# Two weight buffers become one with high and low parts in alternate elements, and the operands beside it move to chosen offsets

## The chip, the cores and the metric

The kernel runs on one core of one Trainium2 chip. The metric is the device time of one execution in microseconds. The kernel before took 3037.07 us, the median of 3 runs (3036.71 to 3037.24).

## The reference

Two transformer-like blocks are computed in float32 for 256 tokens of width 1024, each with two layers. The first block carries a second stream of 256 context tokens; its layers are feed-forward, mixer (a Fourier and gated linear attention mixer in layer 0, a convolution and differential attention mixer in layer 1), feed-forward. The second block has one stream; each of its layers has four branches (state space, three kinds of attention), each projected by `w_branch`, gated by a sigmoid of `h @ w_gate`, summed, projected by `w_out`, and then a feed-forward. Almost all arithmetic is in products of activations with large weight matrices:

```python
def _swiglu(h, w_in, w_out):
    g, u = jnp.split(h @ w_in, 2, axis=-1)
    return (jax.nn.silu(g) * u) @ w_out

proj = jnp.einsum('bsnc,ncd->bsnd', ys, w_branch)
gates = jax.nn.sigmoid(h @ w_gate + b_gate).reshape(bsz, seq, N_BRANCH, D_MODEL)
merged = jnp.sum(gates * proj, axis=2)
return merged @ w_out
```

## The kernel before, in words

Every large product is made from two parts of each operand. A float32 number is split into a high part, rounded to the type fp32r, and a low part, the rest. `three` (L451) then issues three matmuls per tile: high by high, high by low, low by high. Each has its own stationary operand, 128 by 128, and a moving operand of 256 or 512 columns.

Weights come in units of at most 2048 elements per partition. There are two slots (index `s`), each of two halves of 1024 elements (index `h`), so a half holds up to eight tiles of 128 columns and feeds 24 matmuls. For each half, SyncE issues one DMA of up to 512 KB into `raw` (`sp_units`, L372), ScalarE copies it to `whi` (`act_split`, L396), VectorE writes `raw - whi` to `wlo` (`dve_split`, L402), and TensorE multiplies (`pe_blocks`, `pe_tokens`, `beside_block`, `product` and others, all through `half_of`, L457, and `three`). Semaphores count halves: ScalarE may overwrite a half of a slot when TensorE has finished the unit that used it (`mm_done`), DMA may overwrite `raw` when VectorE has made the low part (`lo_ready`).

In most products the weights are the stationary operand and the activations move. In the token-major ones (`pe_tokens`, the "v" units of `beside_block`, L1158, L1408) it is the other way round: the activations are stationary and 256 columns of weights move.

The activations are in three pairs of buffers: `xh`/`xl` (the inputs of the products after a norm or a mixer; 512 elements a row of `k`), `hid_h`/`hid_l` (the hidden layer of a feed-forward) and `h_yh`/`h_yl` (the branch outputs of the second block, 256 elements a row). ScalarE writes the high ones, VectorE the low ones.

All buffers are cut from one slab by hand: a `Region` (L132) hands out addresses one after the other, rounded up to 32 bytes. From the sizes, the buffers of this kernel stand at these bytes of the slab, and at these remainders of 512:

```
whi 43520 (0)   wlo 59904 (0)   hT 76288 (0)   xh 92672 (0)   xl 109056 (0)
hid_h 125440 (0)   hid_l 150016 (0)   h_yh 126112 (160)   h_yl 130208 (160)
```

All tiles of one buffer that a matmul takes (128 or 256 elements on, 2048 bytes on for the next `k` of `xh`) begin at the remainder of their buffer.

Of the kernel before, what the change touches and what calls it, by code (L numbers as in the profile page):

```python
# [20 lines left out]
F32R = mybir.dt.float32r  # L21
# [5 lines left out]
P = 128  # L27
D = 1024
DC = D // P
T = 256  # L30
# [3 lines left out]
UNIT = 2048  # L34
# [88 lines left out]
def build(nc, io, const_at):  # L123

    ctx = ExitStack()
    with ctx:

        SLAB = 212704
        base = (nc.sbuf_base + 31) // 32 * 32
        ctx.enter_context(nc.sbuf_tensor("slab", [P, SLAB // 4], F32))  # L130

        class Region:  # L132
# [5 lines left out]
            def __call__(self, name, shape, dt=F32):  # L138
# [2 lines left out]
                assert self.at <= self.end, (name, self.at, self.end)  # L141
                return t

        fixed = Region(0)
        n_const = max(b for _, b in const_at.values())
        consts = fixed("consts", [P, n_const])
# [14 lines left out]
        post_eps = rstd_col[:, NT:2 * NT]  # L161
        tok_scale = ss[:, T:2 * T]
        raw = fixed("raw", [P, 2, 2, UNIT // 2])
        whi = fixed("whi", [P, 2, 2, UNIT // 2], F32R)
        wlo = fixed("wlo", [P, 2, 2, UNIT // 2], F32R)
        hT = fixed("hT", [P, DC, 2 * T])
        xh_at = fixed.at
        xh = fixed("xh", [P, DC, 2 * T], F32R)
        xl_at = fixed.at
        xl = fixed("xl", [P, DC, 2 * T], F32R)  # L170
        overlay = fixed.at

        first = Region(overlay)
        hid_h = first("hid_h", [P, max(HALVES), 2 * T], F32R)
        hid_l = first("hid_l", [P, max(HALVES), 2 * T], F32R)
        act32 = first("act32", [P, 2, 2 * T])
        hid32 = first("hid32", [P, 2, 2 * T])
        out_at = first.at
        mod_w = first("mod_w", [P, 2, DC, 2 * P])
        mod_row = first("mod_row", [P, 2 * P])  # L180
# [40 lines left out]
        e_kkT0 = ev("e_kkT0", [P, 2, NT, 384])  # L221
        e_S = ev("e_S", [P, 2, 5, 3, P])
        e_xh = Region(xh_at, xl_at)("e_xh", [P, DC, 2 * T])
        e_xl = Region(xl_at, overlay)("e_xl", [P, DC, 2 * T])


        od = Region(overlay + 4 * DC * 2 * T)
# [16 lines left out]
        h_out = Region(out_at)("h_out", [P, DC, T])  # L244
        hy = Region(overlay)
        h_small = hy("h_small", [P, NT, 84])
        h_yh = hy("h_yh", [P, 4, T], F32R)
        h_yl = hy("h_yl", [P, 4, T], F32R)
        h_gates = hy("h_gates", [P, DC, T])
# [3354 lines left out]
```

## Time and profile before

| | before |
|---|---|
| median of 3 runs | 3037.07 us |
| span of the profiled execution | 3035.4 us |
| TensorE busy, matmuls | 2979.4 us (98%) |
| TensorE busy, weight loads | 2629.2 us (87%) |
| VectorE busy | 1691.5 us (56%) |
| ScalarE busy | 1314.2 us (43%) |
| DMA, mean | 145 GB/s |
| mean granted TensorE clock | 0.996 |

The span goes from the first to the last instruction of the core. Busy time of TensorE is modelled: each matmul has a length that includes the way through the array, so consecutive ones overlap, and how often they come is read from their starts. The profile gives no device time of the profiled execution besides its span.

### The profile page before, as it was taken

To read this page: it belongs to the slowest core of one execution; us is meant where nothing else is said; L and a number is where in the kernel's file an instruction comes from. 1 tells how busy PE (TensorE), PEld (TensorE's weight loads), DVE (VectorE), ACT (ScalarE), POOL (GpSimd) and SP (SyncE) were. 2 spreads that over 40 slices of the span, in tenths; PEclk is the share of its full clock that TensorE was granted. 3 is DMA by queue.
4 is the path that set the end of the run, shared out by engine and by line. 5 is a ranking of instruction groups with operands and counts; after the bars stand their busy time and mean duration, and the time that the engine had idled before them with its cause. 6 is when DMAs were issued, how large, how long until landed. Compare 5 with 4: busy or idle time off the path is not lost.

```text
span 3035.4 us, 52037 instructions
## 1 busy us (share of the span) xinstructions
PE 2979.4 (98%) x20172; PEld 2629.2 (87%) x20172; DVE 1691.5 (56%) x2664; ACT 1314.2 (43%) x1952; POOL 0.2 (0%) x4
## 2 busy tenths in 40 slices
PE   8999999999999999999999999999999999999999
PEld 6778878787777878888889999999899999998998
DVE  4333363544332453334666667677766676787666
ACT  4322333423222332223345555555654554556544
POOL 0000000000000000000000000000000000000000
PEclk9999999999999999999999999999999999999999
DMA  9564342055576433333324655455456645554564
GB/s 276 174 185 133 115 146 82 30 167 167 172 212 184 132 100 88 110 90 92 110 71 117 188 167 158 144 155 166 133 159 181 180 124 163 155 155 142 155 183 129
DMA packets 639011, 439.36 MB, mean 145 GB/s; under 512 B 22172, under 2 KB 627192, under 8 KB 638712
## 3 DMA queue, kind: packets, MB, share of 16 engines
q1 hardware_dynamic: 637844, 436.70, 48.3%
q8 instruction: 125, 2.05, 0.3%
q14 instruction: 46, 0.38, 0.0%
q10 hardware_dynamic: 996, 0.23, 0.0%
HBM read 430.84 MB, written 1.05 MB: 142 GB/s over the span
## 4 chain that ended last, share of the span: by engine, by line
PE 88%; DVE 7%; ACT 2%; issue 1%; SPq 1%; DMA 1%; DVEq 0%; ACTq 0%
PE ps L453 27%; PE ps L455 26%; PE ps L454 26%; PE ps L541 2%; DVE wlo L402 2%; ACT whi L396 1%; PE ps L1803 1%; PE ps L1771 1%; DMA raw<-ffn_w_in 1%; DVE normed L2666 1%; PE ps L1791 1%; SPq L717 1%; DVE xl L2658 0%; PE ps L1252 0%; PE ps L1261 0%
## 5 line engine op out<-in xcount | busy, mean ns | idle before, releaser
L453 PE MATMUL ps<-xh,whi 128*128 128x256 f32 (+1 forms) x3744 | 1218.3, 325 | 23.1 <-DVE wlo L402 5.1
L454 PE MATMUL ps<-xl,whi 128*128 128x256 f32 (+1 forms) x3744 | 1197.2, 320 | 0.0
L455 PE MATMUL ps<-xh,wlo 128*128 128x256 f32 (+1 forms) x3744 | 1197.1, 320 | 0.0
L402 DVE TENSOR_TENSOR wlo<-raw,whi 128x1024 fp32r<-128x1024 f32 x732 | 868.9, 1221 | 186.9 <-ACT whi L396 178.2
L396 ACT ACTIVATE whi<-raw 128x1024 fp32r<-128x1024 f32 x731 | 746.5, 1052 | 472.2 <-PE ps L455 412.6
L453 PEld LDWEIGHTS ps<-xh,whi 128*128 128x128 f32 x3744 | 713.8, 191 | 105.3 <-issue 43.4
L455 PEld LDWEIGHTS ps<-xh,wlo 128*128 128x128 f32 x3744 | 714.0, 191 | 50.8
L454 PEld LDWEIGHTS ps<-xl,whi 128*128 128x128 f32 x3744 | 714.7, 191 | 48.8
L453 PE MATMUL ps<-hid_h,whi 128*128 128x512 f32 (+1 forms) x1056 | 355.9, 337 | 0.0
L454 PE MATMUL ps<-hid_l,whi 128*128 128x512 f32 (+1 forms) x1056 | 354.9, 336 | 0.0
L455 PE MATMUL ps<-hid_h,wlo 128*128 128x512 f32 (+1 forms) x1056 | 354.8, 336 | 0.0
L2731 DVE TENSOR_TENSOR hid<-act,ps 128x512 f32<-128x512 f32 (+1 forms) x132 | 73.1, 554 | 460.7 <-PE ps L455 455.5
L2050 ACT ACTIVATE hid_h<-hid 128x256 f32 (+3 forms) x132 | 69.3, 525 | 445.8 <-DVE hid L2731 445.8
L453 PEld LDWEIGHTS ps<-hid_h,whi 128*128 128x128 f32 x1056 | 200.4, 190 | 23.5 <-issue 3.3
L455 PEld LDWEIGHTS ps<-hid_h,wlo 128*128 128x128 f32 x1056 | 200.5, 190 | 20.7
L454 PEld LDWEIGHTS ps<-hid_l,whi 128*128 128x128 f32 x1056 | 200.5, 190 | 20.4
L2782 DVE SCALAR_TENSOR_TENSOR hT<-ps,mod,hT 128x256 f32 (+1 forms) x112 | 49.9, 480 | 214.9 <-PE ps L455 214.6
L2735 DVE TENSOR_TENSOR hid_l<-hid,hid_h 128x256 f32 (+3 forms) x132 | 73.8, 559 | 105.7 <-ACT hid_h L2050 105.7
L2047 ACT ACTIVATE act<-ps 128x512 f32<-128x512 f32 (+1 forms) x88 | 47.6, 541 | 149.9 <-PE ps L455 149.7
L453 PE MATMUL ps<-whi,xh 128*128 128x256 f32 x384 | 111.7, 291 | 0.0
L454 PE MATMUL ps<-wlo,xh 128*128 128x256 f32 x384 | 108.5, 283 | 0.0
L455 PE MATMUL ps<-whi,xl 128*128 128x256 f32 x384 | 108.5, 283 | 0.0
(380 smaller groups left out, 2595.4 us busy)
## 6 DMA issues: line engine op xcount, KB each, us to landing
raw<-ffn_w_in SPq DMA_DIRECT2D x176, 512.0 KB, 4.6
mod_w<-ada_w SPq DMA_DIRECT2D x72, 1024.0 KB, 7.5
raw<-w_in SPq DMA_DIRECT2D x96, 512.0 KB, 4.5
raw<-w_ffn_in SPq DMA_DIRECT2D x88, 512.0 KB, 4.7
raw<-w_gate SPq DMA_DIRECT2D x64, 512.0 KB, 4.0
raw<-ffn_w_out SPq DMA_DIRECT2D x64, 384.0 KB, 4.0
raw<-ffn_w_out SPq DMA_DIRECT2D x64, 320.0 KB, 3.6
raw<-w_branch SPq DMA_DIRECT2D x32, 512.0 KB, 3.4
```

Of the source, the lines that this page charges most:

```text
L396: nc.scalar.activation(whi[:, s, h, :], raw[:, s, h, :], ACT.Copy).then_inc(S("hi_ready"), 1)
L402: nc.vector.tensor_tensor(wlo[:, s, h, :], raw[:, s, h, :], whi[:, s, h, :].bitcast(F32), ALU.subtract).then_inc(S("lo_ready"), 1)
L453: nc.tensor.matmul(dst, w_h, x_h, start=start, stop=False)
L454: nc.tensor.matmul(dst, w_h, x_l, start=False, stop=False)
L455: return nc.tensor.matmul(dst, w_l, x_h, start=False, stop=stop)
L541: m = nc.tensor.matmul(ps[g, bank, 0:2 * P], cond[:, k, 30 - 2 * j:62 - 2 * j], w[:, k, :], start=j == 0 and k < 4, stop=j == n - 1 and k ...
L717: sp.dma_start(norm_tiles[name][j], mod_columns((MOD_UNITS * layer + m0 + j) // MOD_UNITS, (m0 + j) % MOD_UNITS))\
L2047: nc.scalar.activation(act32[:, s, 0:n_tok], gate_in, ACT.Silu).then_inc(S("act_ready"), 1)
L2050: nc.scalar.activation(hid_h[:, bass.ds(i * 2 + (hid0 + s), 1), 0:n_tok], hid32[:, s:s + 1, 0:n_tok], ACT.Copy).then_inc(S("hid_h_ready"), 1)
L2731: nc.vector.tensor_tensor(hid32[:, s, 0:n_tok], act32[:, s, 0:n_tok], ps[:, 2 * s + 1, 0:n_tok], ALU.mult).then_inc(S("evac_done"), 1)
L2735: nc.vector.tensor_tensor(hid_l[:, to, 0:n_tok], hid32[:, s:s + 1, 0:n_tok], hid_h[:, to, 0:n_tok].bitcast(F32), ALU.subtract)\
L2782: ins = nc.vector.scalar_tensor_tensor(out=hT[:, to, sl], in0=ps[:, 2 * s:2 * s + 1, sl], scalar=mod[:, bass.ds(i * 2 + (gate0 + n0 + s), ...
```

## The change

The two weight buffers become one, `w_both`, in which the last index is 0 for the high part and 1 for the low part: an element of the high part stands at every eighth byte, with its low part in the four bytes between. `whi` and `wlo` are views of it, so no instruction is added or removed; every access to them has a step of two elements. `Region.phase(at)` moves the next buffer up until its address leaves the remainder `at` by 512. It is used to put `w_both` at 128, `xh` and `xl` at 256, `hid_h` and `hid_l` at 192, `h_yh` and `h_yl` at 320. The remainders of the activations minus that of the weights are thus 128, 64 and 192. The overlay starts at 128. The buffers grow by the padding alone.

```diff
+            def phase(self, at):
+
+                self.at += (at - base - self.at) % 512
+
+        W_PHASE, X_PHASE, HID_PHASE, HY_PHASE = 128, 256, 192, 320
...
-        whi = fixed("whi", [P, 2, 2, UNIT // 2], F32R)
-        wlo = fixed("wlo", [P, 2, 2, UNIT // 2], F32R)
+        fixed.phase(W_PHASE)
+        w_both = fixed("w_both", [P, 2, 2, UNIT // 2, 2], F32R)
+        whi, wlo = w_both[:, :, :, :, 0], w_both[:, :, :, :, 1]
         hT = fixed("hT", [P, DC, 2 * T])
+        fixed.phase(X_PHASE)
         xh_at = fixed.at
         xh = fixed("xh", [P, DC, 2 * T], F32R)
         xl_at = fixed.at
         xl = fixed("xl", [P, DC, 2 * T], F32R)
+        xl_end = fixed.at
+        fixed.phase(128)
         overlay = fixed.at
 
         first = Region(overlay)
+        first.phase(HID_PHASE)
         hid_h = first("hid_h", [P, max(HALVES), 2 * T], F32R)
...
         hid32 = first("hid32", [P, 2, 2 * T])
+        first.phase(128)
         out_at = first.at
...
-        e_xl = Region(xl_at, overlay)("e_xl", [P, DC, 2 * T])
+        e_xl = Region(xl_at, xl_end)("e_xl", [P, DC, 2 * T])
...
         h_small = hy("h_small", [P, NT, 84])
+        hy.phase(HY_PHASE)
         h_yh = hy("h_yh", [P, 4, T], F32R)
```

## Rows read from the trace of the kernel before

**Rows 1.** The page's first part: busy us, share of the span, instructions.
```profile
PE 2979.4 (98%) x20172; PEld 2629.2 (87%) x20172; DVE 1691.5 (56%) x2664; ACT 1314.2 (43%) x1952; POOL 0.2 (0%) x4
```

**Rows 2.** The chain that ended last, by engine and by line.
```profile
PE 88%; DVE 7%; ACT 2%; issue 1%; SPq 1%; DMA 1%; DVEq 0%; ACTq 0%
PE ps L453 27%; PE ps L455 26%; PE ps L454 26%; PE ps L541 2%; DVE wlo L402 2%; ACT whi L396 1%; PE ps L1803 1%; PE ps L1771 1%; DMA raw<-ffn_w_in 1%; DVE normed L2666 1%; PE ps L1791 1%; SPq L717 1%; DVE xl L2658 0%; PE ps L1252 0%; PE ps L1261 0%
```

**Rows 3.** Matmul groups by form: busy us, mean ns; idle us before, releasers.
```profile
L453 PE MATMUL ps<-xh,whi 128*128 128x256 f32 x2464 | 713.1, 289 | 13.5 <-DVE xl L2697 4.2 <-DVE wlo L402 2.9 <-DVE xl L3471 2.1
L453 PE MATMUL ps<-xh,whi 128*128 128x512 f32 x1280 | 505.2, 395 | 9.6 <-DVE xl L2658 3.4 <-DVE xl L2562 3.0 <-DVE wlo L402 2.3
...
L453 PE MATMUL ps<-hid_h,whi 128*128 128x512 f32 x528 | 206.4, 391 | 0.0
...
L453 PE MATMUL ps<-hid_h,whi 128*128 128x256 f32 x528 | 149.5, 283 | 0.0
...
L453 PE MATMUL ps<-whi,xh 128*128 128x256 f32 x384 | 111.7, 291 | 0.0
...
L453 PE MATMUL ps<-h_yh,whi 128*128 128x256 f32 x256 | 73.3, 286 | 2.5 <-DVE wlo L402 2.3
```

**Rows 4.** Two stretches of 100 us, matmuls alone: length, busy, count, clock, DMA.
```profile
300.00:400.00 100.00, 100.00 (x443) 1.00 0.42 131
...
2300.00:2400.00 100.00, 100.00 (x836) 1.00 0.60 174
```

**Rows 5.** Matmuls on the branch outputs, in order of time: start, us, instruction.
```profile
2053.73 0.28 PE L455 MATMUL ps<-h_yh,wlo 128*128 128x256 f32 x1
...
2054.79 0.28 PE L455 MATMUL ps<-h_yh,wlo 128*128 128x256 f32 x1
```

**Rows 6.** The chain in order of time, plain float32 matmuls: start, us, what.
```profile
1603.08 1.79 PE ps L1507 x16
...
1630.39 1.73 PE ps L863 x8
```

**Rows 7.** Matmuls of 84 moving columns, in order of time.
```profile
1873.73 0.29 PE L455 MATMUL ps<-m_sw_h,xl 128*128 128x84 f32 x1
...
1874.62 0.29 PE L454 MATMUL ps<-m_sw_l,xh 128*128 128x84 f32 x1
```

**Rows 8.** Weight loads of 128, 64 and 32 columns, by form.
```profile
L453 PEld LDWEIGHTS ps<-xh,whi 128*128 128x128 f32 x3744 | 713.8, 191 | 105.3 <-issue 43.4 <-DVE xl L2562 3.1 <-DVE xl L2658 2.2
...
L541 PEld LDWEIGHTS ps<-mod_w,cond 128*32 128x32 f32 x1152 | 33.7, 109 | 29.9 <-issue 8.5 <-DMA mod_w<-ada_w 2.4
...
L1803 PEld LDWEIGHTS ps<-a_pT,a_v 128*64 128x64 f32 x288 | 14.7, 135 | 6.4
```

**Rows 9.** One matmul and the next one's weight load, in order of time.
```profile
299.92 0.39 PE L453 MATMUL ps<-xh,whi 128*128 128x512 f32 x1
299.93 0.19 PEld L454 LDWEIGHTS ps<-xl,whi 128*128 128x128 f32 x1
```

**Rows 10.** The two splits of the weights, by form.
```profile
L402 DVE TENSOR_TENSOR wlo<-raw,whi 128x1024 fp32r<-128x1024 f32 x732 | 868.9, 1221 | 186.9 <-ACT whi L396 178.2 <-issue 0.9 <-ACT whi L1926 0.2
...
L396 ACT ACTIVATE whi<-raw 128x1024 fp32r<-128x1024 f32 x731 | 746.5, 1052 | 472.2 <-PE ps L455 412.6 <-DMA raw<-w_ffn_out 15.0 <-DMA raw<-ffn_w_out 10.5
```

**Rows 11.** Stretches: length; busy of PE, PEld, DVE, ACT, POOL; clock, DMA share, GB/s.
```profile
0.00:20.00 20.00, 16.72 (x107) 13.47 (x107) 7.04 (x12) 8.90 (x15) 0.20 (x4) 1.00 0.97 305
...
1640.00:1832.00 192.00, 190.26 (x1578) 189.47 (x1577) 119.02 (x150) 113.34 (x145) 0.00 (x0) 1.00 0.62 180
...
1960.00:2222.00 262.00, 254.66 (x2111) 236.35 (x2110) 196.73 (x328) 146.88 (x267) 0.00 (x0) 1.00 0.51 153
```

**Rows 12.** The chain within 1960 to 2222 us, by line.
```profile
by line: PE ps L453 22.2%; PE ps L454 20.3%; PE ps L455 20.2%; DVE wlo L402 6.6%; PE ps L1803 3.8%; PE ps L1771 3.8%; PE ps L1791 3.7%; ACT whi L396 3.2%; issue 2.7%; DVE h_gates L3428 1.8%; PE ps L1777 1.6%; DVE a_p L3380 1.1%; DVE a_relu 
```

**Rows 13.** VectorE's weight splits in one of the stretches of rows 11.
```profile
1640.00:1832.00 192.00, 89.90 (x76) 1.00 0.62 180
```

## The prediction, made before the change was run

> **What bounds the kernel now.** I read the page's first part, the chain, the matmul groups, and then the starts of single matmuls in order of time. TensorE is busy for 98% of the span [rows 1] and holds 88% of the chain; the three matmuls of `three` alone are 79% [rows 2]. In most stretches nothing but the pace of TensorE counts, so the question is what one matmul costs from start to start. The mean lengths of 283 and 390 ns [rows 3] do not tell, since consecutive matmuls overlap.
>
> Two stretches of matmuls alone do [rows 4]. In 100 us with 512 moving columns 443 matmuls are counted, two of which only overlap the edges: 100/441 = 226.8 ns each. With 256 columns it is 836, less three: 100/833 = 120.0 ns. The 256 further columns cost 106.8 ns, or 0.417 ns a column, which is the 2.4 GHz level, and the granted clock of both stretches is 1.00. So 256 columns stream in 106.7 ns, 512 in 213.3 ns, and each matmul carries 13.3 to 13.5 ns more. Three rows say that this surplus is not a fixed price:
> - plain float32 matmuls, eight records of 256 columns, take 1.73 us: 216 ns each; sixteen of 128 columns take 1.79 us: 112 ns each [rows 6]. Against 213.3 and 106.7 ns the surplus is 2.9 and 5.2 ns;
> - the split matmuls with 84 moving columns start every (1874.62 - 1873.73)/8 = 111 ns [rows 7]. They stream in 35 ns, so their weight load sets this pace. Loads of 128, 64 and 32 columns last 191, 135 and 109 ns [rows 8], some 0.85 ns a column, so about 107 ns of a load scale with its columns;
> - the matmuls on the branch outputs, same form and 256 columns, start every (2054.79 - 2053.73)/9 = 117.8 ns [rows 5]. Their activations stand 160 bytes off the weights' remainder by 512, all others 0.
>
> A matmul and the load for the next one start together (299.92 and 299.93 [rows 9]). While 128 weights (512 bytes) are read, 256 activations (1024 bytes) are: the moving reads run through addresses at twice the pace of the load and overtake it again and again, from a common remainder. I read the surplus beyond 3 to 5 ns as collisions of these two reads.
>
> **The change part by part.** No instruction comes or goes, no wait, no DMA; each access to `whi` and `wlo` steps by 8 bytes.
>
> *Weights stationary, the interleave.* A load now spans 1024 bytes in the same 107 ns, the pace of the moving reads. Two readers at one pace keep their distance; a first collision delays one of them and is then over. The best that rows show for the pace is 112 ns with 256 columns (two streams of 107 ns [rows 6, 7]), and for 512 columns 213.3 plus 2.9 to 5.3 ns, 216 to 219; I take 217.5. The other end is 120.0 and 226.8, nothing gained, and below it a load that is slowed by the step (rival 3). I take the lower end because the 160-byte offset alone already moved the pace from 120.0 to 117.8, with no other difference in the instruction.
> - 512 columns: 3 x (1280 + 528) = 5424 matmuls [rows 3] x 9.3 ns = 50 us.
> - 256 columns, inputs and hidden: 3 x (2464 + 528) = 8976 x 8.0 ns = 72 us.
> - 256 columns, branch outputs: 3 x 256 = 768 x 5.8 ns = 4 us.
>
> *Weights moving*, 3 x 384 = 1152 matmuls [rows 3]. They now read 2048 bytes in 107 ns against a load of 512 contiguous bytes; four times the pace instead of twice. No row has such a read. The ends are -8 ns each (-9 us) and twice the streaming time, 213 + 5 ns, so +98 ns each (+113 us). I take 0, nearest to today's 120 ns.
>
> *The three distances* (128, 64, 192). Equal pace should make them alike. Were one of them bad, it would forfeit its own term: branch outputs 4 us, hidden 3 x 528 x (9.3 + 8.0) = 27 us, inputs the rest.
>
> *The splits.* VectorE takes 1221 ns and ScalarE 1052 ns for 1024 elements a partition [rows 10], a little over one element a cycle; strided writes and one strided read should leave that. Ends: unchanged, or a doubled VectorE split, 732 x 1.2 = 890 us more VectorE work. In the densest feed-forward stretch, 1640 to 1832 us, VectorE is busy 119 of 192 us [rows 11], so some 10% more would be hidden, a doubling would not. I take 0.
>
> *What is late next.* A half feeds 24 matmuls: 2.88 us now, 2.69 us then, against 1.22 us of VectorE and 1.05 us of ScalarE for it. DMA moves 180 GB/s in 1640 to 1832 us and would need 193; 305 were moved at the start [rows 11]. Both keep their cover. In the two attention stretches (1960 to 2222 us and its twin of the other layer) the `three` lines hold only 63% of the chain, the splits 10% [rows 12]. About 1620 of the matmuls lie in each, worth 13 us each; I let a third of these 26 us be lost to VectorE and ScalarE: 8 us back.
>
> *Sum.* 50 + 72 + 4 - 8 = 118 us: 3035.4 - 118 = 2917 us of span. The median is 1.7 us above the span, so 2919 us; I say 2920.
>
> The Trainium skill, "SBUF — State Buffer", section "Door 1: The DMA port swizzle", states 16-byte cachelines with at least two hits a line for full bandwidth. A step of 8 bytes gives exactly two float32 hits, so by this rule neither load nor splits slow down and the sum stands; no row of this trace has such a step.
>
> **The rivals.**
> 1. *Collisions only half relieved*: equal pace with a persistent touch, or one distance bad. For it: the 160-byte offset gave only 2.2 of 8 ns. Half of the 126 us gives 2975 us.
> 2. *The surplus is the price of an fp32r matmul*, and the offset effect is small: everything stays, 3037 us, at best -5 us. For it: 120.0 and 226.8 carry the same 13.3 ns, as a fixed price would. Against it: [rows 5, 7] have the same kind of matmul at 117.8 and 111 ns. By the Trainium skill, "TensorE: Matmul & The Clock Gate", Part 2, step 1, the streaming operand and the weight load have independent read ports and do not take bandwidth from each other; that is this rival, and [rows 4, 5] speak against it.
> 3. *The 8-byte step slows the reads of TensorE* (slower than before). A load whose variable part grows by a factor f takes 5 + 107f ns; with 256 columns it decides as soon as that passes 120 ns, f above 1.07. At f = 2 it is 219 ns, 99 ns on each of 9744 matmuls, +965 us, less 50 us of the 512-column gain: about 3950 us. With 512 columns the load would still be hidden. A milder case: only the moving reads of weights double, +113 us against the gain of 118: 3032 us. If besides that half of the gain is missing it is slower, 3095 us. For it: twice as many lines of memory are touched for the same data. Against it: each load column now takes 0.85 ns, two columns of streaming, so the memory has already twice the rate to give.
> 4. *VectorE's or ScalarE's split slows by half or more.* In 1640 to 1832 us the 76 splits take 89.9 of VectorE's 119 us [rows 11, 13], so beside 1.18 us of split a half costs it 0.38 us, and TensorE needs 192/76 = 2.53 us for one (2.36 after the change). A split half as long again makes 2.15 us, still hidden; a doubled one 2.75 us, 9% over today's pace of the 256-column stretches. These hold 3 x 3632 matmuls of 120 ns, 1308 us: +110 us, about 3150 us.
>
> **How the numbers follow.** Full relief 0.45, half relief or one bad case among the terms 0.25, no change 0.08, rival 3 in some form 0.15, rival 4 0.07. Faster by over 0.2% (6 us; about what a measurement of this kernel tells from no change): 0.45 + 0.25 = 0.70. Same 0.08, slower 0.22. Low end: all 512-column matmuls at 216, weights moving at 112, nothing lost in attention: 126 + 8 + 9 = 143, so 2894; a little more for the plain tail, 2885. The high end reaches over half relief and no change to the mild slower case, 3060. The likeliest case's own range is 2885 to 2960.
>
> **What would show it.** Starts of split matmuls 112 ns apart with 256 columns and 216 to 219 with 512, in the stretches of [rows 4]; branch outputs at 112 instead of 117.8. The weight load still 191 ns, the splits still 1221 and 1052 ns. If hidden and inputs differ in pace, the distance matters. A matmul count per 100 us that stays 443 and 836 shows rival 2; loads longer than 200 ns show rival 3; DVE `wlo` above 1.3 us shows rival 4. Weights moving at more than 120 ns would show the unknown term.

## The result: slower by 5.4%

The changed kernel took 3201.61 us (median of 4 runs, 3200.53 to 3202.1) against 3037.15 us before on the same chip, a ratio of 1.0541 (95% interval 1.0526 to 1.0556). The prediction said 2920 us. The profiled execution has a span of 3198.7 us, 163.3 more than before.

The page's first part and the chain of the changed kernel, which answer to [rows 1, 2]. Lines 465 to 467 are now the three matmuls of `three`, L414 and L408 the splits.

```profile
PE 3148.1 (98%) x20172; PEld 2786.0 (87%) x20172; DVE 1694.1 (53%) x2664; ACT 1381.8 (43%) x1952; POOL 0.2 (0%) x4
...
PE 91%; DVE 5%; ACT 1%; issue 1%; DMA 1%; SPq 0%; DVEq 0%; ACTq 0%
```

TensorE is 168.7 us busier, a little more than the whole loss; its share of the chain rose from 88 to 91%. VectorE works as long as before, ScalarE 68 us longer. The groups by form (busy us, mean ns, idle before) say where:

```profile
L465 PE MATMUL ps<-xh,w_both 128*128 128x256 f32 x2464 | 717.0, 291 | 12.7 <-DVE xl L2709 4.3 <-DVE w_both L414 3.0 <-DVE xl L3483 2.1
...
L465 PE MATMUL ps<-xh,w_both 128*128 128x512 f32 x1280 | 509.0, 398 | 9.5 <-DVE xl L2670 3.4 <-DVE xl L2574 3.1 <-DVE w_both L414 2.1
...
L465 PE MATMUL ps<-hid_h,w_both 128*128 128x512 f32 x528 | 209.7, 397 | 0.0
...
L465 PE MATMUL ps<-w_both,xh 128*128 128x256 f32 x384 | 161.6, 421 | 0.0
...
L414 DVE TENSOR_TENSOR w_both<-raw,w_both 128x1024 fp32r<-128x1024 f32 x732 | 869.2, 1221 | 221.6 <-ACT w_both L408 219.5 <-issue 0.4 <-ACT w_both L1938 0.2
...
L408 ACT ACTIVATE w_both<-raw 128x1024 fp32r<-128x1024 f32 x731 | 816.2, 1152 | 487.9 <-PE ps L467 438.5 <-DMA raw<-ffn_w_in 11.8 <-DMA raw<-w_ffn_out 11.1
...
L465 PEld LDWEIGHTS ps<-xh,w_both 128*128 128x128 f32 x3744 | 735.5, 196 | 99.5 <-issue 43.0 <-DVE xl L2574 2.9 <-DVE h_out L535 2.2
```

Against [rows 3], the matmuls in which the weights move went from 291 to 421 ns; no other form of that group changed by more than 6 ns. Against [rows 8] the load is 196 instead of 191 ns. Against [rows 10], VectorE's split stayed at 1221 ns and ScalarE's rose from 1052 to 1152.

Again the starts give the pace. First the changed kernel's count in 100 us with 512 moving columns (length, busy, count, clock, DMA share, GB/s), then two of its matmuls with moving weights, fourteen starts apart:

```profile
300.00:400.00 100.00, 100.00 (x433) 1.00 0.43 133
```

```profile
499.67 0.41 PE L465 MATMUL ps<-w_both,xh 128*128 128x256 f32 x1
...
502.87 0.41 PE L467 MATMUL ps<-w_both,xl 128*128 128x256 f32 x1
```

100/431 = 232.0 ns per matmul, against 226.8 in [rows 4]; and (502.87 - 499.67)/14 = 228.6 ns where weights move, against 120 before. Summed over the start-to-start intervals of the trace, the 1152 matmuls with moving weights cost 123 us more, those with 512 columns 24 us more, those with 256 columns and stationary weights 14 us more: 161 of the 163 us. All other matmuls together changed by some 2 us.

One stretch of the same trace tells what kind of limit the moving weights met. From 491.5 to 494.9 us the granted clock was 0.50, the 1.2 GHz level:

```profile
491.60:494.80 3.20, 3.20 (x15) 0.50 0.76 222
```

The matmuls in it, all with moving weights, came every 229.8 ns, against 228.6 ns at a clock of 1.00 just after. (In the run with the interleaving alone, below, such a stretch gave 236.6 ns.) With stationary weights and 256 contiguous moving columns, 56 matmuls of this trace fell wholly into stretches at 0.50; they came at a median of 213 ns, against 120 at 1.00. So the contiguous stream follows the granted clock, and the read with a step of 8 bytes hardly does: it has a pace of its own, slower than both.

### The profile page after: what moved, and what is told of

Read it like the earlier page. It is cut to its first block, busy times and chain, and to the rows that moved or that the text cites. A ratio compares the mean times of both kernels' runs of the same rounds, so it can differ in the third digit from the quotient of the medians.

```text
span 3198.7 us, 52037 instructions
## 1 busy us (share of the span) xinstructions
PE 3148.1 (98%) x20172; PEld 2786.0 (87%) x20172; DVE 1694.1 (53%) x2664; ACT 1381.8 (43%) x1952; POOL 0.2 (0%) x4
## 4 chain that ended last, share of the span: by engine, by line
PE 91%; DVE 5%; ACT 1%; issue 1%; DMA 1%; SPq 0%; DVEq 0%; ACTq 0%
PE ps L465 28%; PE ps L467 27%; PE ps L466 27%; PE ps L553 2%; DVE w_both L414 1%; ACT w_both L408 1%; PE ps L1815 1%; PE ps L1783 1%; PE ps L1803 1%; DVE normed L2678 1%; DVE xl L2670 0%; PE ps L1264 0%; PE ps L1273 0%; PE ps L1480 0%; PE ps L1503 0%
## 5 line engine op out<-in xcount | busy, mean ns | idle before, releaser
L465 PE MATMUL ps<-xh,w_both 128*128 128x256 f32 (+1 forms) x3744 | 1225.9, 327 | 22.2 <-DVE w_both L414 5.1
L467 PE MATMUL ps<-xh,w_both 128*128 128x256 f32 (+1 forms) x3744 | 1206.2, 322 | 0.0
L466 PE MATMUL ps<-xl,w_both 128*128 128x256 f32 (+1 forms) x3744 | 1205.3, 322 | 0.0
L408 ACT ACTIVATE w_both<-raw 128x1024 fp32r<-128x1024 f32 x731 | 816.2, 1152 | 487.9 <-PE ps L467 438.5
L414 DVE TENSOR_TENSOR w_both<-raw,w_both 128x1024 fp32r<-128x1024 f32 x732 | 869.2, 1221 | 221.6 <-ACT w_both L408 219.5
L465 PEld LDWEIGHTS ps<-xh,w_both 128*128 128x128 f32 x3744 | 735.5, 196 | 99.5 <-issue 43.0
L467 PEld LDWEIGHTS ps<-xh,w_both 128*128 128x128 f32 x3744 | 733.9, 196 | 45.9
L466 PEld LDWEIGHTS ps<-xl,w_both 128*128 128x128 f32 x3744 | 733.2, 196 | 44.1
L465 PE MATMUL ps<-hid_h,w_both 128*128 128x512 f32 (+1 forms) x1056 | 359.5, 340 | 0.0
L466 PE MATMUL ps<-hid_l,w_both 128*128 128x512 f32 (+1 forms) x1056 | 358.3, 339 | 0.0
L467 PE MATMUL ps<-hid_h,w_both 128*128 128x512 f32 (+1 forms) x1056 | 358.3, 339 | 0.0
L465 PEld LDWEIGHTS ps<-hid_h,w_both 128*128 128x128 f32 x1056 | 207.4, 196 | 23.3 <-issue 3.3
L467 PEld LDWEIGHTS ps<-hid_h,w_both 128*128 128x128 f32 x1056 | 207.3, 196 | 20.2
L465 PE MATMUL ps<-w_both,xh 128*128 128x256 f32 x384 | 161.6, 421 | 0.0
L466 PE MATMUL ps<-w_both,xh 128*128 128x256 f32 x384 | 159.9, 417 | 0.0
```

Of the source, the lines that this page charges most:

```text
L408: nc.scalar.activation(whi[:, s, h, :], raw[:, s, h, :], ACT.Copy).then_inc(S("hi_ready"), 1)
L414: nc.vector.tensor_tensor(wlo[:, s, h, :], raw[:, s, h, :], whi[:, s, h, :].bitcast(F32), ALU.subtract).then_inc(S("lo_ready"), 1)
L465: nc.tensor.matmul(dst, w_h, x_h, start=start, stop=False)
L466: nc.tensor.matmul(dst, w_h, x_l, start=False, stop=False)
L467: return nc.tensor.matmul(dst, w_l, x_h, start=False, stop=stop)
```

## The experiments

*Distance* is the address of the moving operand minus that of the stationary one, in bytes, by 512 or by 256. *Pace* is the time from the start of one matmul to the start of the next. A *place* is a run of 16 bytes that begins at a multiple of 16, so four float32. The diffs of the first three experiments and of the last are against the changed kernel.

Two theories stood against each other for the stationary weights. Mine (A): the moving read and the weight load meet, and their distance decides. B: the surplus over 112 ns is not theirs, and distance does nothing. For the moving weights: the 8-byte step itself, or the place.

### The offsets alone

```diff
-        w_both = fixed("w_both", [P, 2, 2, UNIT // 2, 2], F32R)
-        whi, wlo = w_both[:, :, :, :, 0], w_both[:, :, :, :, 1]
+        whi = fixed("whi", [P, 2, 2, UNIT // 2], F32R)
+        wlo = fixed("wlo", [P, 2, 2, UNIT // 2], F32R)
```

> The weights' high and low parts stay in two contiguous buffers; only the offsets of the change are made (weights at remainder 128, inputs 256, hidden 192, branch outputs 320 by 512). Theory A: the surplus of a split matmul over 112 ns comes from the moving read and the weight load meeting, and their distance matters with contiguous weights: the 256-column matmuls on inputs and hidden come every 117 to 118 ns instead of 120.0, as those on the branch outputs did before with a distance of 160, the 512-column ones some 2 ns sooner than 226.8: 8976 x 2.3 + 5424 x 2 = 31 us less, about 3006 us. Theory B: the distance does nothing and the branch outputs were faster for another reason: 120.0 and 226.8 stay, 3037 us.

3048.73 us, ratio 1.0038 (1.0024 to 1.0052): neither theory's time, slower than before by 12 us. The trace shows both signs: branch outputs (distance 192) came every 115 ns in the mean, most of them 113 to 114, hidden parts (64) every 118, inputs (128) every 119; but with 512 columns hidden parts came at 229 and inputs at 232 instead of 226.8. Summed over the starts, the matmuls with 512 columns lost 22 us and all others gained 12. Distance matters, in opposite directions for the two widths. In the changed kernel's place, 300 to 400 us, the count is that of the changed kernel, without interleaving:

```profile
300.00:400.00 100.00, 100.00 (x433) 1.00 0.43 136
```

### The interleaving alone

```diff
-        W_PHASE, X_PHASE, HID_PHASE, HY_PHASE = 128, 256, 192, 320
+        W_PHASE, X_PHASE, HID_PHASE, HY_PHASE = 128, 128, 128, 288
```

> The interleaved buffer alone; the distances of inputs and hidden to it by 512 are 0 and that of the branch outputs 160, as in the kernel before. Theory A (a load and a moving read at one pace keep their distance, so the distance decides): with distance 0 they are in each other's way all the time, the 256-column matmuls come at over 126 ns and the 512-column ones at over 236; over 3250 us. Theory B (the distance does nothing): as the changed kernel, 3202 us, with weights moving at 229 ns. Theory C (no equal pace matters, only the number of places touched): also 3202 us within 10 us.

3201.57 us, ratio 1.0539 (1.0521 to 1.0557): the time of the changed kernel. Theory A's blow-up at distance 0 did not come; the 512-column matmuls came every 233 to 234 ns, the 256-column ones at 120. So the interleaving alone makes the whole loss. The equal times hide a small exchange: summed over the starts, the 512-column matmuls lost 34 us here and 24 in the changed kernel, the 256-column ones with stationary weights 6 here and 14 there. The three distances saved 10 us in one form and cost 8 in the other. Nor do the two halves of the change add up: with 512 columns the offsets alone cost 22 us, the interleaving alone 34, both together 24.

### Moving weights read in one run

```diff
+        def run_of(s, h, j):
+            return w_both[:, s, h, :, :].rearrange("p n j -> p (n j)")[:, j * 512:j * 512 + 256]
...
-                              w_h[:, j, :], w_l[:, j, :], k == 0, k == kc - 1)
+                              run_of(s, 2 * k // kc, j), run_of(s, 2 * k // kc, j), k == 0, k == kc - 1)
```

> The changed kernel, but in the 1152 token-major matmuls, where the weights move, they read 256 consecutive elements of the interleaved buffer (high and low parts mixed, so these products are not the reference's) instead of every second one. If the 8-byte step of the moving read is what costs there, their pace goes from 229 to about 120 ns, 1152 x 109 = 125 us less: 3077 us. If it is the place or the concurrent writes into the same buffer, it stays near 229 ns and 3202 us. In either case the other split matmuls keep the surplus of the changed kernel (232 ns with 512 columns, 120 to 122 with 256), some 37 us over before.

The diff shows one of four places with the same edit. The sums of these products leave out the splitting: they mix high and low parts.

3076.72 us, ratio 1.0132 (1.0115 to 1.0149): 125 us under the changed kernel, the figure expected. The group of 384 is back at its old length:

```profile
L465 PE MATMUL ps<-w_both,xh 128*128 128x256 f32 x384 | 111.9, 292 | 0.0
```

Same buffer, same writes into it: the 8-byte step of the moving read costs 125 of the 164 us. The other 40 us stay, as expected, with the stationary weights.

### Series of one matmul

The kernel before, and behind its end series of 24 equal matmuls, each series on its own line, such as

```python
for _ in range(24): nc.tensor.matmul(ps[:, 7, 0:256], fw[:, 0:128], fx[:, 48:304], start=True, stop=True)  # s1 m1 D192
```

with `fw` the flat `whi` and `fx` the flat `xh`.

> The kernel before, and behind its last instruction of TensorE 90 series of 24 fp32r matmuls each, which read the weight and the input buffers at chosen distances and steps (s1 m1: both contiguous; s2: stationary step of two elements; m2: moving step of two; and so on). Theory A: with both contiguous the pace of a series depends on the distance by 512: 120 ns at 0, 117 to 118 at 160, and somewhere near 112; with the stationary step of two it depends on it more strongly. A moving read that touches twice the 16-byte places takes about twice as long (step 2 and 4-byte pairs in 16 alike), while blocks of four elements out of eight cost nothing. Theory B: only the element step counts: blocks of four cost as much as step 2, and distance does nothing. A stationary step of 4 or 8 elements shows what the load itself costs: if it is still 112 ns with 64 moving columns, the load has room; if it doubles, step 2 was the last that was free.

The chain in order of time (start, us, what) shows each series as a piece; a twenty-fourth of it is the pace. L1909, L1911, L1917, L1919 and L1925 are distances 0, 32, 192, 256 and 448 with 256 columns, all contiguous. L1928 is distance 0 with 512 columns, L1930 128 and L1932 192. L1941 and L1948 have a stationary step of two elements at distances 0 and 192, L1953 the same with 512 columns. L1959 has a moving step of two, L1965 of four, L1966 of eight; L1967 moves two elements of four, L1968 four of eight. L1971 and L1972 have stationary steps of three and four, L1978 a stationary step of four and 64 moving columns.

```profile
3030.60 3.55 PE ps L1909 x24
...
3037.01 2.80 PE ps L1911 x24
...
3054.01 2.75 PE ps L1917 x24
...
3059.60 2.87 PE ps L1919 x24
...
3076.67 2.73 PE ps L1925 x24
...
3085.05 5.48 PE ps L1928 x24
...
3096.05 5.59 PE ps L1930 x24
...
3107.25 5.59 PE ps L1932 x24
...
3141.17 2.88 PE ps L1941 x24
...
3161.33 2.88 PE ps L1948 x24
...
3175.75 5.59 PE ps L1953 x24
...
3209.17 5.52 PE ps L1959 x24
...
3239.37 5.60 PE ps L1965 x24
3244.97 5.23 PE ps L1966 x24
3250.19 5.44 PE ps L1967 x24
3255.64 2.83 PE ps L1968 x24
...
3264.06 4.17 PE ps L1971 x24
3268.23 5.67 PE ps L1972 x24
...
3297.38 5.58 PE ps L1978 x24
```

(The first series begins at a granted clock of 0.50, until 3032 us; from then on its starts are 120 ns apart.) What they say:
- Contiguous, 256 columns: 120 ns at distance 0 and 256, 117 at 32, 114 at 192 and 448. The pattern has a period of 256 bytes. The series at 512 took 2.86 us, those at 1024, 1536, 2048, 4096 and 8192 took 2.88 us each, 120 ns.
- Contiguous, 512 columns: 228 at 0, 233 at 128 and 192. Here 0 is good.
- Stationary step of two: 120 at 0 and at 192 with 256 columns, 118 to 121 over the twelve distances tried, and 230 to 233 with 512. Distance has lost most of its power.
- Moving step of two: 5.52/24 = 230 ns. Two of four costs as much (227), four of eight nothing (118), so it is not the gap between elements that costs. But neither does each further place of 16 bytes: steps of three, four and eight, with one or two elements used of each 16 bytes or one of every 32, took 227, 233 and 218 ns. The moving read has two paces here, one for full places and one, about twice as long, for half-used or emptier ones.
- A stationary step of three takes 174 ns, of four 236, of eight 241: step two was the last that a load could nearly take.

The series with 64 to 224 columns fell partly into stretches in which the granted clock was 0.50, the 1.2 GHz level (3288 to 3326 us, once a series of 64 columns had run before it, and 3353 to 3363 us). Their paces are used only for this: L1978 lies wholly at 0.50 and took 232 ns a matmul, as much as a load with a step of four at 1.00 (L1946 below, 233 ns). The load with a wide step, too, keeps a pace that does not follow the granted clock.

### Which reader costs what

The same with other series.

> The kernel before with another 65 series behind its end. The floor of each reader: a stationary step of 0 or a moving step of 0 takes away the new places that this reader touches. Theory A (the surplus is the two readers meeting): with either step 0 the pace is 112 to 113 ns with 256 columns, and with 512 columns about 216 to 219 ns, 8 to 11 below the 227 of two real readers; a moving step of 2 with stationary step 0 stays near 220, as it costs by itself. Theory B (a fixed price of the split matmul): 512 columns stay at 227 with either step 0. Distances of 0 to 240 with 512 columns show a minimum other than 0 under 222 ns only if the repeated overtaking can be avoided there; theory A expects none, since 2048 bytes of moving reads pass all places many times. The three matmuls of the kernel in their real order at distance 0 and 192 should give 120 and 113 to 114 ns.

In the chain, L1938 has 512 columns with a moving step of 0, L1934 the same with a stationary step of 0 and real moving reads. With 256 columns and a moving step of 0 the stationary step is 0 (L1942), 1 (L1943), 2 (L1944), 3 (L1945), 4 (L1946). L1948 and L1951 have a stationary step of 0 and real moving reads at distances 0 and 192. L1926 is distance 240 with 512 columns. L1957 and L1962 have 240 moving columns, both operands contiguous, at distances 0 and 192.

```profile
3116.34 5.45 PE ps L1926 x24
...
3141.80 5.55 PE ps L1934 x24
...
3164.03 5.25 PE ps L1938 x24
...
3185.54 2.69 PE ps L1942 x24
3188.22 2.69 PE ps L1943 x24
3190.91 2.83 PE ps L1944 x24
3193.74 4.17 PE ps L1945 x24
3197.90 5.60 PE ps L1946 x24
...
3209.21 2.74 PE ps L1948 x24
...
3217.43 2.74 PE ps L1951 x24
...
3233.94 2.70 PE ps L1957 x24
...
3248.15 2.70 PE ps L1962 x24
```

With 256 columns theory A holds: either reader held to one place gives 112 to 114 ns, so the 6 ns above are the two together, and distance 192 avoids them. But the interleaved load needs 2.83/24 = 118 ns with nothing to meet. With steps of 2, 3, 4 and 8 (5.71 us) the load of 128 columns touches 64, 96, 128 and 128 places of 16 bytes, which makes 1.8 to 1.9 ns a place in all four: an estimate from these series. By it a contiguous load with its 32 places is far from this limit, and a load with a step of two has just reached it. With 512 columns theory A fails in part: 5.25/24 = 219 ns only when the moving read stands still; with the load held to one place it is 5.55/24 = 231 ns, above the 227 of two real readers. Of the sixteen distances by 16 bytes, 0 and 240 gave 227, the others 229 to 235 (means of the later starts). The 6 ns belong to 256 columns: with 240 the pace was 2.70/24 = 112.5 ns at distance 0 and at 192 alike. The three matmuls in their real order and with both parts gave 120.0 at distance 0 and 113.3 at 192 (means of the last 48 starts), and 226.7 and 233.3 with 512 columns.

### A layout from the series

Contiguous weights; distance 0 while 512 columns move; from the last feed-forward of the first block on, where 256 move, the inputs and hidden parts are placed 192 bytes further, and the branch outputs too.

```diff
+        xh = Moved(pair_of("xh", xh, xh_at, [P, DC, 2 * T]))
+        xl = Moved(pair_of("xl", xl, xl_at, [P, DC, 2 * T]))
+        hid_h = Moved(pair_of("hid_h", hid_h, hid_h_at, [P, max(HALVES), 2 * T]))
+        hid_l = Moved(pair_of("hid_l", hid_l, hid_l_at, [P, max(HALVES), 2 * T]))
...
+        def staged(schedule):
+            Moved.now = 0
+            for entry in schedule:
+                if entry[:3] == ('gains', 1, 2):
+                    Moved.now = 1
+                yield entry
```

(`...` stands for lines left out here.) `Moved` hands out the first buffer of a pair or the one 192 bytes on, by `Moved.now`; each engine's loop runs over `staged(schedule)`.

> Contiguous weights as in the kernel before, everything at remainder 0 for the stages with 512 moving columns; from the second feed-forward of layer 1 of the first block on, where 256 columns move, inputs and hidden parts stand 192 bytes further, and so do the branch outputs. The series measured 113.3 ns against 120.0 with 256 columns at a distance of 192, and 227.3 at distance 0 with 512 columns as the best there. Theory A (the distance by 256 bytes sets the surplus): about 8000 weight-stationary matmuls save 6.6 ns and 768 branch ones 4 ns, 56 us, of which some 8 are lost between other engines: about 2988 us, faster than both kernels. Theory B (the series, in which one pair of addresses repeats, does not carry over to the real order of reads): under 15 us of it arrives, over 3020 us.

2997.0 us against 3037.55, ratio 0.9863 (0.9844 to 0.9882): faster than both kernels. And as a control the same with 256 in place of 192:

> The same kernel with inputs and hidden parts moved by 256 bytes instead of 192 (branch outputs at 192 as in the other). Theory A with a period of 256 bytes: as at distance 0, 120.0 ns; only the branch outputs gain, 3 us: about 3034 us. Theory C (the period is 512 or more, or it is the move itself that helps): it gains like the other, below 3010 us.

3033.54 us, ratio 0.9989 (0.9979 to 0.9999): inputs and hidden parts stayed at 120.0, most of the branch outputs came at 113 to 114. So it is the distance by 256 and not the move. The counts of the two, the 192 one in two stretches, then the 256 one:

```profile
2240.00:2275.00 35.00, 35.00 (x311) 1.00 0.67 193
...
1740.00:1780.00 40.00, 40.00 (x342) 1.00 0.64 186
```

```profile
2260.00:2300.00 40.00, 40.00 (x336) 1.00 0.59 169
```

Less the three that only overlap the edges, 35/308 = 113.6 and 40/339 = 118.0 ns, against 40/333 = 120.1. The gain is 41 us and not the 56 at which the expectation put the matmuls, because some stretches stay at 118 at the same distance: of 8888 moved matmuls in the trace 3346 came 116 to 119 ns apart, and together they all took 15 us more than at a pace of 113.4. The 8 us that the expectation gave away to other engines were not lost. One of the stretches at 118 begins in the middle of a product; the chain there (start, us, what), in which some 0.2 us are lost around 2374.97:

```profile
2374.74 0.11 PE ps L498
2374.86 0.11 PE ps L499
2374.97 0.33 PE ps L497
2375.30 0.12 PE ps L498
2375.42 0.12 PE ps L499
```

Before the gap the starts are 113 and 114 apart, after it 117 to 119 until the product ends. So two paces exist at distance 192. The traffic does not tell them apart: the two stretches above moved 193 and 186 GB/s. Nor does it take a gap: among the series, `three` with the parts swapped (the inputs stationary at 64, the weights moving at 0, so again 192 by 256) came every 117.8 ns from its beginning (L1969), and the same `three` with stationary weights every 113.3 (L1967). What decides was not tried and stays open.

## Why the prediction was wrong, by its steps

*What bounds the kernel*: right. The pace of one matmul was the whole story: from start to start, the matmuls outside `three` took 414 us against 413 before, and the idle time before the inputs' matmuls stayed (12.7 and 9.5 us against 13.5 and 9.6 in [rows 3]).

The forecast missed by 282 us. Of these 164 lie in the step on stationary weights, 123 in the one on moving weights, and 8 go the other way.

*Weights stationary, the interleave* (50 + 72 + 4 us gained): this step failed, and with it the sign. It took 112 ns and 217.5 ns as the paces that two readers at equal speed would reach. Measured were means of 119 to 121 and of 231 to 233, 38 us lost in place of 126 gained. Three things were wrong in it:
- The floor of 112 ns was one of contiguous loads [rows 6, 7]. It is real for these (L1943 above), but a load with step two takes 118 by itself (L1944). The prediction gave the load unlimited room for the step on the argument that two streamed columns fit into one load column. Step three at 174 ns shows how little room there was. In the terms of rival 3, 5 + 107f, the load's f was 1.06, just under the 1.07 from which it was to decide.
- For 512 columns the surplus was read as collisions. It is not cured by taking the load's places away (231 ns, L1934), only by letting the moving read stand still (219, L1938). The 2.9 ns of plain float32 matmuls was the wrong comparison, since these took 216/256 = 0.84 ns a column and not 0.417.
- Equal pace was to make distance harmless for the better; it left the 256-column pace at 119 to 121 in the mean of every form, and in the series at 118 to 121 wherever the operands stood.

What was right in it: that the 117.8 ns of [rows 5] came from the offset of 160 bytes (117.4 in the series at 160, L1916). Distance was a lever worth 6 ns, but for contiguous weights.

*Weights moving* (0 taken, -9 to +113 us as ends): the size was off, and it is most of the loss. 229 ns a matmul, +123 us in the trace and 125 by experiment, 10 us beyond the upper end. Taking "nearest to today's 120 ns" had no row behind it; the end of the range was the mechanism.

*The three distances alike*: right in the total (3201.6 us without and with them beside the interleaving), partly by luck, since 10 us saved with 512 columns and 8 us lost with 256 cancel.

*The splits*: VectorE 1221 ns as said. ScalarE's grew by 100 ns, which the prediction had not allowed for; it was hidden, since the starts of the matmuls account for the loss without it. *Sum*: 8 us were given back for attention stretches that gained nothing. Two slips in the working carry nothing: 0.85 ns for 128 columns make 109 ns and not 107, and 732 x 1.2 us are 878 and not 890.

*Rivals.* The third, an 8-byte step that slows the reads of TensorE, is what happened, in its milder form: the moving reads double, the load takes 6 ns more. It was given 0.15, with 3095 us for the form in which half of the gain is missing too; what was missing was all of it and 38 us more. The upper end of the range, 3060 us, left that form out. Its sign, loads longer than 200 ns, did not show either (196), because the moving read slowed and not the load. The second rival (the surplus belongs to any fp32r matmul, distance does little) is wrong: with either reader held to one place, or at distance 192, 256 columns lost most of their surplus (112 to 113.4 ns). For 512 columns it is right in that no layout tried removed the surplus, and 226.7 ns at distance 0 was the best with two real readers.

The Trainium skill, "SBUF — State Buffer", section "Door 1: The DMA port swizzle", gives full bandwidth from two hits on a line of 16 bytes. The measurement decides otherwise for the moving operand: two of four elements used take 227 to 230 ns, all four 118 to 120. Its line of 16 bytes itself agrees with the series: four of eight in a block cost nothing. VectorE's split, with one read and its write at this step, agrees with the rule (1221 ns before and after); ScalarE's write does so only nearly (1152 against 1052). The Trainium skill, "TensorE: Matmul & The Clock Gate", Part 2, step 1, has the two readers independent. The series with 256 columns disagree at distance 0 (120.0 ns, against 113.4 with the load held to one place) and agree at 192 (113.3).

## What to carry to other kernels

In this kernel's fp32r matmuls an operand that is streamed has to use whole 16-byte places; half-used ones doubled the time of the stream, and a stationary operand with a step of more than two elements became the bound. The distance by 256 bytes between moving and stationary operands is a free parameter worth up to 5% of a 256-column fp32r matmul, nothing at 240 columns, and with another optimum at 512: measure a series per form before laying out memory. A floor read from rows holds only for the access pattern of those rows.

## What the runs showed of the hardware that was not expected

- With 512 columns, a real load at distance 0 (227 ns) is better than one that reads a single place (231 ns). This was not explained.
- The effect of distance is sharp: 113.3 ns at 192, and 120.0 at 184 and at 200.
- The same code at the same distance runs at 113.3 or at 117.8 ns; in one place the change came with a gap of 0.2 us.
- A read that uses half of its places or fewer hardly follows TensorE's clock: 229.8 ns at a granted clock of 0.50 and 228.6 at 1.00 for the moving one.
